# A two-block transformer kernel in fp32: the weight slots around each norm multiplied in two halves of 256 tokens

## The reference

```python
# first block
h = modulate(rmsnorm(x, norm1_g), shift1, scale1)             # n1 -> h1
qa, ka, va, qb, kb, vb, ga, gb = split(h @ w_in)
merged = sigmoid(ga) * (swa(qa, ka, va) @ w_branch_a) + sigmoid(gb) * (moba(qb, kb, vb) @ w_branch_b)
x = x + gate1 * (merged @ w_out)
h = modulate(rmsnorm(x, norm2_g), shift2, scale2)             # n2 -> h2
x = x + gate2 * (square(relu(h @ w_mlp_in)) @ w_mlp_out)      # 1024 -> 4096 -> 1024
x = rmsnorm(x, final_g)                                       # n3
# second block, two layers; alpha = sqrt(2)
h = modulate(x, sh1, sc1)                                     # h3
x = layer_norm(alpha * x + g1 * short_conv(h))                # n4
x = layer_norm(alpha * x + g2 * swiglu(modulate(x, sh2, sc2)))  # n5, hidden width 2816
k, v, log_f = projections of modulate(x, kv_shift, kv_scale)  # h5; log_f is the forget gate
x = layer_norm(alpha * x + g1 * forgetting_attention(modulate(x, sh1, sc1)))  # hq; n6
x = layer_norm(alpha * x + g2 * swiglu(modulate(x, sh2, sc2)))  # n7, the output
```

## Time and profile before

| what | value |
|---|---|
| median of 3 runs | 2064.57 us (2061.17 to 2064.68) |
| the profiled execution | 2063.71 us, of which the span from the first to the last instruction is 2061.9 us |
| PE busy | 1948.4 us, 94% |
| DVE, ACT, POOL busy | 1180.6 us (57%), 755.6 us (37%), 335.9 us (16%) |
| mean granted clock of TensorE | 0.978 |
| chain of waits that ended last | PE 66%, DVE 6%, ACT 4% |

### The profile page before, as it was taken

One profiled execution on the slowest core, in us unless ns is written; L12 is line 12 of the kernel. 1 busy time (PEld: TensorE's weight loads), 2 busy tenths in 40 slices (PEclk: granted clock), 3 DMA queues, 4 the chain that ended last, 5 costly groups with the idle time before them and its releaser, 6 DMA issues.

```text
span 2061.9 us, 22454 instructions
## 1 busy us (share of the span) xinstructions
PE 1948.4 (94%) x9048; PEld 1601.6 (78%) x9048; DVE 1180.6 (57%) x1865; ACT 755.6 (37%) x1141; POOL 335.9 (16%) x297
## 2 busy tenths in 40 slices
PE   4999999899999989998999999989998889999996
PEld 2888888788888878876788888768887668888884
DVE  6566555576667646467645644665666553433436
ACT  4566522342222234223322222364566342222223
POOL 4423111011111102004000000236222130000002
PEclk9999999999999999998999999989999989999998
DMA  9422465265656424431655433232111213323321
GB/s 331 130 80 67 138 235 195 82 252 197 224 188 220 143 82 184 163 103 41 245 184 180 166 103 102 82 103 87 41 42 41 82 61 103 102 82 102 102 82 41
DMA packets 126121, 267.55 MB, mean 130 GB/s; under 512 B 4464, under 2 KB 33152, under 8 KB 126017
## 3 DMA queue, kind: packets, MB, share of 16 engines
q1 hardware_dynamic: 121056, 248.59, 35.2%
q0 software_dynamic: 4960, 17.53, 2.3%
HBM read 261.84 MB, written 8.45 MB: 131 GB/s over the span
## 4 chain that ended last, share of the span: by engine, by line
PE 66%; DVE 6%; ACT 4%; issue 1%; ACTq 0%; DVEq 0%
PE ps L599 21%; PE ps L601 21%; PE ps L600 21%; DVE t L1568 1%; DVE t L1542 1%; DVE t L1559 1%; DVE t L1556 1%; ACT t L1157 1%; PE ps L714 1%; DVE t L1602 1%; ACT t L1063 1%; DVE t L1513 1%; ACT t L1111 1%; DVE t L1505 0%; PE ps L677 0%
## 5 line engine op out<-in xcount | busy, mean ns | idle before, releaser
L599 PE MATMUL ps<-t 128*128 128x512 f32 (+1 forms) x2584 | 1004.6, 389 | 33.7 <-DVE t L1542 15.9
L600 PE MATMUL ps<-t 128*128 128x512 f32 (+1 forms) x2584 | 996.5, 386 | 0.0
L601 PE MATMUL ps<-t 128*128 128x512 f32 (+1 forms) x2584 | 996.5, 386 | 0.0
L599 PEld LDWEIGHTS ps<-t 128*128 128x128 f32 x2584 | 488.5, 189 | 139.0 <-issue 25.4
L1445 DVE TENSOR_TENSOR t<-t 128x2048 fp32r<-128x2048 f32 x133 | 305.7, 2298 | 461.8 <-ACT t L1063 461.8
L601 PEld LDWEIGHTS ps<-t 128*128 128x128 f32 x2584 | 488.0, 189 | 103.0
L600 PEld LDWEIGHTS ps<-t 128*128 128x128 f32 x2584 | 488.2, 189 | 97.9 <-issue 1.0
L1063 ACT ACTIVATE t<-t 128x2048 fp32r<-128x2048 f32 x133 | 254.2, 1911 | 613.7 <-PE ps L601 609.8
L1457 DVE CUSTOM_DVE_ANT_0 t<-t 128x1024 f32<-128x1024 f32 x144 | 175.5, 1260 | 9.7 <-DMA t<-in_ada 4.1
L1505 DVE SCALAR_TENSOR_TENSOR t<-ps,t 128x512 f32<-128x512 f32 x184 | 132.4, 747 | 83.9 <-PE ps L601 75.5
L1568 DVE TENSOR_TENSOR t<-ps,t 64x512 fp32r<-64x512 f32 (+4 forms) x183 | 103.8, 578 | 103.4 <-ACT t L1189 48.7
(11 more groups left out here) (158 smaller groups left out, 1432.5 us busy)
## 6 DMA issues: line engine op xcount, KB each, us to landing
t<-in_ada SPq DMA_DIRECT2D x48, 1024.0 KB, 5.8
t<-in_gate SPq DMA_DIRECT2D x22, 1024.0 KB, 5.1
t<-in_up SPq DMA_DIRECT2D x22, 1024.0 KB, 5.1
t<-in_down SPq DMA_DIRECT2D x22, 1024.0 KB, 5.0
t<-in_w_in SPq DMA_DIRECT2D x17, 1024.0 KB, 6.1
t<-in_w_mlp_in SPq DMA_DIRECT2D x16, 1024.0 KB, 5.4
t<-in_w_mlp_out SPq DMA_DIRECT2D x16, 1024.0 KB, 5.0
t<-in_ada_t POOLq DMA_DIRECT2D x13, 1024.0 KB, 5.9
```

What stands on the lines that cost most here:

```text
L599: pe.matmul(o, wh, xh, start=first, stop=False)
L600: pe.matmul(o, wh, xl, start=False, stop=False)
L601: return pe.matmul(o, wl, xh, start=False, stop=last)
```

## The change

For the norms n2 to n7 the two slots ahead of the norm and (but for n7) the two slots behind it are multiplied in two halves z = 0 and 1 of 256 tokens each, with half-width products. The k-tiles are taken in pairs p = 0 to 3. `EARLY` says how many pairs are already complete when the last two slots begin (2 at n2, n4, n6, whose other tiles come from earlier slots; 0 at n3, n5, n7).

- `last_halves`: both slots for z = 0, then both for z = 1. After half of the tiles of the first slot in z = 1 come the sums of half 0 (`norm_sums(site, 0)`), after that slot the diagonals (`norm_roots(site, 0)`).
- `first_halves`: z = 0 over all 8 k-tiles, with the sums of half 1 behind k-tile 2 and its diagonals behind k-tile 4; then z = 1, k-tiles 0 to 3 (which ends the first slot), then tile by tile k-tiles 4 to 7 (which ends the second). `at_end("pe", s)` of stages 2, 3, 4, 5 and 7 now stands behind `first_halves`.
- Residuals are added by half (operands of 256), all other steps of the norm by pair and half (operands of 2 x 256). ACT, DVE and POOL each get a `norm_halves` with the order of these steps written out. For `EARLY` pairs the sums of squares are added ahead (`early_adds`).
- Both slots behind a norm are pieced, not just the second. `norm_shift` moves forward: at n4 into the last gate slots of the convolution, at n5 and n7 into the last gate slot.
- w_mlp_out for f = 7 was multiplied k by k in its first slot and is now tile by tile, as every half tile is. The tiles behind n2 to n6 (relu, copy, silu, queries) are evacuated in halves (`halves_out`). h5 is modulated through 2 buffers instead of 3. The output is stored in 8 transfers of 256 KB. The memory of a norm is 9 buffers of 128 x 512 instead of 6.

```diff
 PIECED = {0, 1} | set(range(4, 12)) | set(range(AT_FOX + 3, AT_O + 2)) | {
-    s + 1 for s in (AT_MLP, AT_CONV, AT_FFN, AT_Q, AT_LAST)}
+    s + i for s in (AT_MLP, AT_CONV, AT_FFN, AT_Q, AT_LAST) for i in range(2)}
+HALF = [slice(0, 256), slice(256, 512)]
+EARLY = {"n2": 2, "n3": 0, "n4": 2, "n5": 0, "n6": 2, "n7": 0}
...
+            def norm_sums(site, z, layer):
+                m, (bq, _, bd) = norm_mem[site], NORM_BANK[z]
+                q = psum[bq]
+                claim(bq)
+                on.wait_ge(d_norm, "acc", site, z, 3)
+                for i in range(2):
+                    for t in range(2):
+                        ins = pe.matmul(q[:, 2 * z + i:2 * z + i + 1], m["acc"][z][:, blocks[2 * t + i]], ones[:, 0:1],
+                                        start=t == 0, stop=t == 1, skip_group_check=True)
...
+            def last_halves(site, layer, slots, src, key, what):
+                early = EARLY[site]
+                taken = [take(*s[0]) for s in slots]
+                for z in range(2):
+                    for s, (_, tiles, kts) in enumerate(slots):
+                        slot_lo(on, taken[s])
+                        for at, t in enumerate(tiles):
+                            one = early and len(tiles) == 4
+                            tile_half(taken[s], z, t, kts, src, OUT_BANK[early][z][t // 2], not one or s == 0, not one or s == 1,
+                                      (*key, "half", z, t), (x_res, (*what, t, z)))
+                            if (z, s) == (1, 0) and at == len(tiles) // 2 - 1:
+                                norm_sums(site, 0, layer)
+                        if (z, s) == (1, 0):
+                            norm_roots(site, 0)
...
+            def first_halves(site, layer, w, c0, src, key, done):
...
+                for kt in range(8):
+                    for i in range(4):
+                        step(0, i, kt)
+                    if kt == 2:
+                        norm_sums(site, 1, layer)
+                    if kt == 4:
+                        norm_roots(site, 1)
+                for kt in range(4):
+                    for i in range(4):
+                        ins = step(1, i, kt)
+                ins.then_inc(mm.sem, mm.up("slot", taken[0]))
+                for i in range(4):
+                    for kt in range(4, 8):
+                        step(1, i, kt)
+                mm.also("slot", taken[1])
...
-            norm_finish("n2", False, d_norm, "times")
-            at_end("pe", 2, mm)
...
+                if f == 0:
+                    first_halves("n2", False, "w_mlp_in", 0, of_half("h2"), ("mi", 0),
+                                 lambda z, i: (a_evac, ("mi", 0, i, z)))
+                    at_end("pe", 2, mm)
...
+            def norm_halves(site, name, layer, gate, mod, event, before):
...
+                for p in range(e, 4):
+                    residuals(0, p)
+                    if p > max(e, 1):
+                        add(site, 0, p - 1)
+                add(site, 0, 3)
+                diagonal(site, 0, layer)
+                normed(site, name, layer, 0, 0)
+                residuals(1, 0)
+                normed(site, name, layer, 0, 1)
+                low(site, name, 0, 0)
+                residuals(1, 1)
+                low(site, name, 0, 1)
+                if not e:
+                    add(site, 1, 1)
+                normed(site, name, layer, 0, 2)
+                residuals(1, 2)
+                residuals(1, 3)
+                add(site, 1, 2)
+                add(site, 1, 3)
+                low(site, name, 0, 2)
+                normed(site, name, layer, 0, 3)
+                diagonal(site, 1, layer)
```

773 lines of the change are left out of this document (466 added, 307 removed).

## The result

The changed kernel takes 2118.74 us (median of 4, 2117.87 to 2119.41) against 2063.67 us for the kernel before: a ratio of 1.0255, interval [1.0242, 1.0268]. It is 55 us slower; the forecast was 2075 with a range to 2088. The sign was right, the size wrong by more than four times.

What follows compares the result with a forecast made beforehand. The prediction took TensorE's matmul stream (busy 94% of the span) as the bound; new against old windows at n2 to n7 summed to about +12 us on 2063.7, 2075.7, stated as 2075, range 2061 to 2088.

Steps and rivals of the forecast that it cites:

- The wait at the end of the stage: Behind n3, n4, n6: ACT converts the next slot only after both slots' last product; PE stands 4.3, 4.5, 4.3 us.
- n6's second slot: Ahead of n6: PE wants the second slot 5.7 us sooner, DVE is done at 1643.3 at best; wait 8.4 us.
- The sums at n7: At n7 nothing lies behind the norm to hide DVE's work; PE waits 6.1 us for the second half's sums.
- The price of halving: 256-wide instead of 512-wide products in the norm windows: 0.4 us a norm, 2 us in all.
- Rival (d): Half-width products on PE are bound by their weight load, 0.072 us more each, 152 us: 2216; chance 0.01.
- rival (c): Four conversions behind stage_end don't hold PE: 19.5 us and 7 of low clock go, 2049; with variants, chance 0.08.
- the low clock: PE at its lower clock level after a stall: 1.7 to 2 us charged each, 13 us in all.
- the wait behind n2: First product behind n2's two slots waits for the conversion, then act tile 0: 6.4 us.
- the waits for the sums: Inside the windows PE waits for the second half's sums: 1.5 (n2), 2.6 (n3), 2.9 (n4, n6), 3.3 us (n5).
- Rival (a): DVE and POOL hold each other up (1.1 instead of 0.9 us), clock falls after each sums' wait: 2087; chance 0.15.
- Waits behind it: Forecast part on PE's waits after each norm's window, called the term that decides: 4.3 to 6.4 us at n2, n3, n4, n6.
- the gate's wait: Behind n5: lo of the last h5 tile comes some 5.5 us later than PE asks for it for the forget gate.

## Why the prediction was right or wrong

**Right.** The sign, and four waits with their mechanism and size. The wait at the end of the stage: forecast 4.3, 4.5, 4.3 us at n3, n4, n6, measured 4.33, 4.57, 4.33. n6's second slot: 8.4 against 7.84. The sums at n7: 6.1 against 6.7. The act tile ahead of n3: 2.2 against 2.3. The price of halving: 2 against 3 us, step 0.1177. Rival (d) is out, though the weight loads are recorded at 191 to 192 ns each. The stage's end alone was worth 28 us in the run that moved it, about what rival (c) had for it (19.5 and 7). But it did not decide the sign, although the forecast had it so: without this term the sum would have come out below the kernel before, while the measured kernel without it is still 26 us above (2090.74 against 2064.99).

**Wrong: the sum's size.** Against 11.5 us forecast for the six windows stand 49.2. The step that failed is the pricing of the waits and of the clock behind them: the low clock (13 us charged, 27.6 measured), the wait behind n2 (6.4, 11.1) and the waits for the sums at the layer norms. By the terms:

- *The low clock.* I charged 13 us in all, once or twice a norm. Measured are 27.6, against 12.0 before. The price for one was nearly right (1.7 to 2 us; 2.3 to 2.6), the count was not: the chip's clock also fell behind the 2.1 and 2.7 us at n3, behind the waits of 4 to 5 us for the sums at n4, n5 and n6, and twice where PE had hardly waited. Rival (a) had those behind the sums, with 0.8 us a time, where the products lost 0.7 to 1.6; they are 3.3 of the 14.6 us that were missing. The matmuls of the norms ran slow in them too (n7: 10.0 us where I took 4.0 for the second half and 3.2 for the first).
- *The wait behind n2*, 6.4 in "Waits behind it": 11.1. I followed ACT and left out what DVE has ahead of the act tile's lo half, two ada sums whose loads hang on the same wait at SP.
- *The waits for the sums*, 2.6, 2.9, 3.3, 2.9 at n3 to n6: 2.5, 4.2, 4.8, 4.2 beyond a product's step. The chain through ACT's pieces was right; at the layer norms the two sums took 1.43 us each instead of 0.9, and at n3, where POOL does no totals, 0.7. L1513's mean of 0.898 mixes the two: 21 of the 49 took 0.69, at n1, n2 and n3, and the 28 at the layer norms, beside POOL's totals, took 0.68 to 1.57, the last one always 1.56 or 1.57. So the price stood in the trace of the kernel before. The sum laid out in the text, 11.9 against 9.9 us, also gives 2.0 for n4 and not the 2.9 that was used. In the trace L1743's two took 2.87 us at n4 while POOL worked. By the Trainium skill (SBUF — State Buffer, Who interferes with whom) the two take turns on one port, and the trace agrees; I had quoted the rule and then priced by the mean.
- *h2's mark*: a wait of 2.7 us at n3 that I had not seen, since I looked for waits that the diff adds and this line is not in it. It was right when the norm stood behind all products.
- *n5*: the gate's wait 7.0 instead of 5.5, and 4.8 for the sums; 8.2 us instead of 0. The forecast let the gate wait for the last h5 tile; it waited for its PSUM bank, which came free 1.2 us behind that tile.
- *The shift matmuls*: 0.5 us charged, at n5 alone; moved, they cost 0.9 each at n4, n5 and n7.
- *n7*: 5.6 instead of 0.1, with nearly the same wait, but its matmuls at the low clock.

No single term carries the miss. The largest is the low clock, 14.6 of the 37.7 us; nearly each of the others was too small too, because each was laid out with mean durations and a full clock. Some 6 us of the 37.7 I can't put down to a term. My range took the two upper bounds, longer sums and more low clock, and stopped at 2088; the contended row (1.1) was itself too low.

## What to carry to other kernels

When work is split so that one half hides beside the other, look for every mark that meant "all of it is done" and ask who waits for it: the end of a stage and the end of a buffer's use stood behind the halved products and cost 28 and 2 us, and neither wait was new. Ask the same of each PSUM bank. In an order written by hand, place what can start early (the weight pieces, some 17 us) ahead of what must wait. And price operations that will run beside another engine by their contended rows, and each wait of PE of more than 2 us with its stretch of low clock.
